# First modulation of a fused three-block network: two of its four units halved between VectorE and TensorE, its weight laid out by units

## The reference, cut to what matters

```
def _modulation(c, ada_w, ada_b):
    mod = jax.nn.silu(c) @ ada_w + ada_b            # c 1 x 1024, ada_w 1024 x 3072
    shift, scale, gate = jnp.split(mod[:, None, :], 3, axis=-1)
    return shift, scale, gate
...
h = _rmsnorm(x, norm_g[i]) * (1.0 + scale) + shift
proj = h @ w_in                                     # 512 x 1024 times 1024 x 4096
```

## Time and profile before

| | us |
|---|---|
| median of 3 runs | 1538.32 (1538.28 to 1540.69) |
| profiled execution, its own time | 1538.38 |
| span of that execution in the trace | 1536.5 |
| PE busy | 1382.3 (90% of the span) |
| DVE busy | 684.7 (45%) |
| ACT busy | 356.0 (23%) |
| POOL busy | 111.6 (7%) |
| moved by DMA | 338.08 MB, 220 GB/s over the span |

### The profile page before, as it was taken

The page is one execution under the profiler, slowest core; times in us unless marked ns, Lnnn a source line. Parts: engine busy times, 40 slices in busy tenths (PEclk is TensorE's granted clock), DMA queues, the critical chain, the costliest instruction groups (busy, mean ns, idle before and its releaser), DMA issues.

```text
span 1536.5 us, 17675 instructions
## 1 busy us (share of the span) xinstructions
PE 1382.3 (90%) x6712; PEld 699.3 (46%) x6712; DVE 684.7 (45%) x1313; ACT 356.0 (23%) x778; POOL 111.6 (7%) x227
## 2 busy tenths in 40 slices
PE   4999999999999999999999989979996968769685
PEld 2444444555464444664644445455443324223242
DVE  4675524884266723332599845263121112111125
ACT  2433204653220253431500154110000000000001
POOL 4000000010100000000200000112000001000003
PEclk9999999999999999999999989989998989989898
DMA  9763136004176741003424123169999999999995
GB/s 341 261 245 125 55 110 127 4 1 164 52 254 224 237 164 56 1 1 110 148 99 161 58 110 156 64 236 396 419 410 418 420 415 417 416 418 423 423 425 238
DMA packets 85133, 338.08 MB, mean 220 GB/s; under 512 B 10343, under 2 KB 16280, under 8 KB 72376
## 3 DMA queue, kind: packets, MB, share of 16 engines
q1 hardware_dynamic: 70752, 307.24, 51.5%
q0 software_dynamic: 5664, 13.70, 3.2%
q10 hardware_dynamic: 8632, 15.99, 2.9%
HBM read 323.34 MB, written 17.24 MB: 222 GB/s over the span
## 4 chain that ended last, share of the span: by engine, by line
PE 69%; DMA 15%; DVE 9%; issue 2%; ACT 2%; POOL 1%; DVEq 0%; SPq 0%; ACTq 0%; POOLq 0%
PE score_banks L723 14%; PE bank L734 13%; DMA slots<-in_w_exp_up 12%; PE score_banks L1214 9%; PE score_banks L734 5%; PE bank L1241 5%; PE bank L707 3%; PE bank L941 3%; PE score_banks L1228 2%; PE bank L896 2%; PE bank L1043 2%; PE score_banks L1034 2%; DVE bufD L2050 2%; PE score_banks L953 1%; PE bank L957 1%
## 5 line engine op out<-in xcount | busy, mean ns | idle before, releaser
L723 PE MATMUL score_banks<-slots 128*128 128x512 f32 (+1 forms) x584 | 243.3, 574 | 3.0 <-PE score_banks L723 1.5
L1214 PE MATMUL score_banks<-slots,norm_row 128*64 128x512 f32 (+1 forms) x672 | 147.2, 607 | 42.4 <-DMA slots<-in_w_exp_up 42.2
L734 PE MATMUL bank<-slots 128*128 128x512 f32 x416 | 183.2, 594 | 2.2 <-PE bank L734 0.9
L723 PEld LDWEIGHTS score_banks<-slots 128*128 128x128 f32 x584 | 110.4, 191 | 129.6 <-issue 126.8
L2540 DVE TENSOR_TENSOR mix<-probsT,score_banks 128x256 f32<-128x256 f32 (+1 forms) x39 | 14.4, 370 | 287.7 <-ACT probsT L1688 287.7
L1241 PE MATMUL bank<-slots,mix 128*64 128x512 f32 (+1 forms) x864 | 115.2, 477 | 12.0 <-issue 9.5
L734 PEld LDWEIGHTS bank<-slots 128*128 128x128 f32 x416 | 77.5, 190 | 96.6 <-issue 95.0
L1688 ACT ACTIVATE probsT<-score_banks 128x256 f32<-128x256 f32 (+1 forms) x39 | 13.4, 343 | 436.9 <-PE score_banks L1214 376.5
L1214 PEld LDWEIGHTS score_banks<-slots,norm_row 128*64 128x64 f32 (+1 forms) x672 | 49.9, 142 | 133.9 <-issue 132.5
L734 PE MATMUL score_banks<-slots 128*128 128x512 f32 (+1 forms) x256 | 95.2, 527 | 0.3 <-PE score_banks L734 0.3
L2427 DVE SCALAR_TENSOR_TENSOR bufD<-slots,col,bufD 128x512 f32<-128x512 f32 x120 | 80.5, 746 | 0.4
(11 more groups left out here) (376 smaller groups left out, 1767.4 us busy)
## 6 DMA issues: line engine op xcount, KB each, us to landing
slots<-in_w_exp_down SPq DMA_DIRECT2D x32, 2048.0 KB, 35.6
slots<-in_w_exp_gate SPq DMA_DIRECT2D x32, 2048.0 KB, 29.5
slots<-in_w_exp_up SPq DMA_DIRECT2D x32, 2048.0 KB, 34.7
slots<-in_w_in SPq DMA_DIRECT2D x16, 2048.0 KB, 9.0
slots<-in_w_mod SPq DMA_DIRECT2D x24, 1024.0 KB, 5.2
slots<-in_ada_w SPq DMA_DIRECT2D x18, 1024.0 KB, 6.4
slots<-in_w_out SPq DMA_DIRECT2D x6, 2048.0 KB, 8.2
slots<-in_ada_w SPq DMA_DIRECT2D x3, 2048.0 KB, 20.5
```

The lines of the kernel that those rows point to most:

```text
L723: last = mm(bank[:, cols], w[:, k, lo:lo + P], src[:, k, cols], start=(k == 0), stop=(k == kts - 1))
L734: last = mm(bank[:, 0:cols], features_k[:, t * P:(t + 1) * P], rhs(k), start=(k == 0), stop=(k == kts - 1))
L1214: last = mm(out, rows[:, k, :], e_gu[it.p][:, :, k, c * pc.ff:(c + 1) * pc.ff], start=(k == 0), stop=(k == KT - 1))
```

## The change

- On the host, ada_w0 (1024 x 3072) is laid out again as six units of 128 partitions x 8 rows x 512 columns, so that one partition's part of a unit is one run of 16 KB, and of a half unit one of 8 KB. No loads are added or taken away, and their order stays.
- Units 1 and 3 are halved: four of the eight rows on DVE, four on PE. PE's half (`half_unit`) takes the weight's 128x128 blocks as the stationary operand and silu(c)'s column as the one moving column: 16 matmuls, adding up over the four rows, into four columns of a bank. DVE's half is reduced as before, into four further columns of the same bank (`reduce_columns(bank, 4)`), and `take_halves` adds both and the bias with two DVE ops.
- `row_unit`, ACT's copy of the row and six of the 19 warming matmuls go.
- DVE weighs unit 0, four rows of unit 1, scales x, takes unit 0's columns, weighs unit 2 with the taking of unit 1 in its midst, then four rows of unit 3.
- `unit_used` goes up by one after unit 0, after unit 1 is taken and after unit 2 (before: one, then two at once). The first of the two steps of `mod_used` now comes from PE's half of unit 3, the second from DVE once that has been reached.

```diff
         def source(kind, u):
-            if kind in ("ada0", "ada1"):
-                w = a["ada_w0" if kind == "ada0" else "ada_w1"]
+            if kind == "ada0":
+                return a["ada_w0"][u]
+            if kind == "ada1":
+                w = a["ada_w1"]
                 return w[:, u * W:(u + 1) * W].rearrange("(p k) n -> p k n", p=P)
...
-            def reduce_columns():
+            def reduce_columns(bank=None, at=0):
...
-                pe.wait_ge(mod_summed, summed(n))
-                bank = dve_banks.claim(pe)
+                pe.wait_ge(mod_summed, n + 1)
+                bank = dve_banks.claim(pe) if bank is None else bank
                 for j in range(4):
-                    last = mm(bank[:, j:j + 1], mod_acc(n)[:, j * P:(j + 1) * P], ones[:, 0:1], start=True, stop=True)
+                    last = mm(bank[:, at + j:at + j + 1], mod_acc(n)[:, j * P:(j + 1) * P], ones[:, 0:1], start=True, stop=True)
...
-            def row_unit():
...
+            def half_unit(bank, rows, first):
+
+
                 for j in range(4):
-                    last = mm(bank[:, j:j + 1], mod_acc(1)[0:1, j * P:(j + 1) * P], ones[0:1, 0:1], start=True, stop=True)
-                last.then_inc(dve_filled, 1)
-                reduced[0] += 1
+                    for k in range(4):
+                        last = mm(bank[:, j:j + 1], rows[:, k, j * P:(j + 1) * P], silu_c[:, first + k:first + k + 1],
+                                  start=(k == 0), stop=(k == 3))
+                return last
...
             table_columns(0, R1_ROWS)
-            reduce_columns()
-            row_unit()
+            bank0, bank1 = dve_banks.claim(pe), dve_banks.claim(pe)
+            pe.wait_ge(silu_ready, 1)
+            pe.wait_ge(w_in[1], unit_arrival(1))
+            half_unit(bank1, unit_view(1)[:, 4:8], 4)
+            reduce_columns(bank0)
+            reduce_columns(bank1, 4)
             pe.wait_ge(xn_ready, TT)
             for k in range(KT):
                 transposes(act_banks, act_filled, [C_tok[:, t, k * P:(k + 1) * P] for t in range(TT)])
-            reduce_columns()
-            stay_warm(6)
-            reduce_columns()
+            bank2, bank3 = dve_banks.claim(pe), dve_banks.claim(pe)
+            pe.wait_ge(mod_in[0], 16)
+            half_unit(bank3, mod_half[0], 0).then_inc(mod_used, 1)
+            reduce_columns(bank2)
+            reduce_columns(bank3, 4)
             stay_warm(13)
...
             table_column(col1, R1_ROWS)
-            bank = tr_banks.take(act)
-            fn(mod_acc(1)[0:1, :], bank[0:1, :], ACT.Copy).then_inc(tr_freed, 1)
-            act.wait_ge(tr_freed, tr_banks.n)
-            act.sem_inc(row_copied, 1)
...
+            def weigh_second_unit():
+
+                dve.wait_ge(w_in[1], unit_arrival(1))
+                for k in range(4):
+                    chain(weigh_rows(1, k, unit_view(1)[:, k, :]))
+                dve.sem_inc(mod_summed, 1)
+
+            def weigh_third_unit(halfway):
+
+                dve.wait_ge(w_in[2], unit_arrival(2))
+                dve.wait_ge(mod_reduced, 1)
+                for k in range(KT):
+                    if k == 4:
+                        halfway()
+                    chain(weigh_rows(2, k, unit_view(2)[:, k, :]))
+                dve.sem_inc(mod_summed, 1)
+
+            def weigh_fourth_unit():
+
+                dve.wait_ge(mod_in[1], 16)
+                dve.wait_ge(mod_reduced, 2)
+                for k in range(4, KT):
+                    chain(weigh_rows(3, k, mod_half[1][:, k - 4, :], first=4))
+                dve.sem_inc(mod_summed, 1)
+                halves_done[0] = 2
...
+            def take_halves(n, layer, u, bias_col):
+
+                bank = dve_banks.take(dve)
+                part = mods[layer][:, 4 * u:4 * u + 4]
+                chain(v.tensor_tensor(part, bank[:, 0:4], col1[:, bias_col + 4 * u:bias_col + 4 * u + 4], ALU.add))
+                v.tensor_tensor(part, bank[:, 4:8], part, ALU.add).then_inc(dve_freed, 1)
                 dve.wait_ge(dve_freed, dve_banks.n)
                 dve.sem_inc(mod_reduced, 1)
...
             dve.wait_ge(silu_ready, 1)
-            weigh_unit(0)
+            weigh_first_unit()
             dve.sem_inc(unit_used, 1)
+            weigh_second_unit()
             scale_x(0)
             dve.wait_ge(act_freed, 1)
             take_columns(0, 0, 0, R1["ada_b0"])
-            weigh_unit(2)
-            take_columns(1, 0, 1, R1["ada_b0"])
-            dve.sem_inc(unit_used, 2)
-            weigh(3)
+
+            def second_unit_done():
+
+                take_halves(1, 0, 1, R1["ada_b0"])
+                dve.sem_inc(unit_used, 1)
+
+            weigh_third_unit(second_unit_done)
+            dve.sem_inc(unit_used, 1)
+            weigh_fourth_unit()
             take_columns(2, 0, 2, R1["ada_b0"])
-            take_columns(3, 0, 3, R1["ada_b0"])
+            take_halves(3, 0, 3, R1["ada_b0"])
+            dve.wait_ge(mod_used, 1)
+            dve.sem_inc(mod_used, 1)
             affine(0, R1["norm_g0"], col1)
...
+    given["ada_w0"] = np.ascontiguousarray(given["ada_w0"].reshape(P, KT, 3 * D // W, W).transpose(2, 0, 1, 3))
```

More of the change, by code:

```diff
@@ L283, in mod_acc @@
             return buf[:, lo + n % 2 * W:lo + (n % 2 + 1) * W]
-        def summed(n):
-            return n if n > 0 else 1
         def c_loads():
@@ L327, in fused_kernel @@
         mod_in = [sem(f"mod_half_loaded{i}") for i in range(2)]
-        row_copied = sem("second_unit_row_copied")
         mod_used, mod_summed, mod_reduced = sem("mod_half_used"), sem("mod_unit_summed"), sem("mod_unit_reduced")
@@ L2043, in _, with weigh_rows, weigh_first_unit @@
             sums_done, halves_done = [0], [0]
-            def weigh_rows(n, k, w):
+            def weigh_rows(n, k, w, first=0):
                 c = silu_c[:, (0 if n < 12 else 8) + k:(0 if n < 12 else 8) + k + 1]
                 acc = mod_acc(n)
-                if k == 0:
+                if k == first:
                     return v.tensor_scalar(acc, w, c, None, ALU.mult)
                 return v.scalar_tensor_tensor(out=acc, in0=w, scalar=c, in1=acc, op0=ALU.mult, op1=ALU.add)
[L2052 to L2056, removed]
+            def weigh_first_unit():
+                dve.wait_ge(w_in[0], unit_arrival(0))
                 for k in range(KT):
-                    chain(weigh_rows(n, k, unit_view(n)[:, k, :]))
+                    chain(weigh_rows(0, k, unit_view(0)[:, k, :]))
                 dve.sem_inc(mod_summed, 1)
+            def weigh_second_unit():
[18 more added lines that the diff above has]
+                halves_done[0] = 2
             def weigh_half(n, half):
@@ L2083, in take_columns @@
                                 ALU.add).then_inc(dve_freed, 1)
+                dve.wait_ge(dve_freed, dve_banks.n)
+                dve.sem_inc(mod_reduced, 1)
+            def take_halves(n, layer, u, bias_col):
[3 more added lines that the diff above has]
+                v.tensor_tensor(part, bank[:, 4:8], part, ALU.add).then_inc(dve_freed, 1)
                 dve.wait_ge(dve_freed, dve_banks.n)
```

## The result

The changed kernel takes 1554.56 us (median of 4 runs, 1553.32 to 1555.46) against 1538.30 beside it: ratio 1.0114, interval 1.0102 to 1.0126. It is slower, by 16.3 us between the medians. The forecast was 1554, with a range of 1545 to 1563.

The account below looks back on a forecast made before the run. The start-up chain before PE's projection at 45.85 us was in play. A bias table at 33.0, then PE's steps and warming, put the projection at 61.7, 15.9 later: 1538.38 + 15.9 = 1554.3, taken as 1554, range 1545 to 1563.

Parts of the forecast that it names:

- Turns by record: Load queues SP and ACT alternate record by record, so 16 KB ada_w0 records delay the bias table from 19.43 to 33.0.
- its two bounds: Margins on the bias table's landing at 33.0 us: -2.0 and +1.5.
- Unit 0 early, and worth nothing: Unit 0's weight lands at about 10 us, without gain, as DVE weighs until about 20, then waits to scale x.
- PE's clock: PE's one-column work: 1.2 GHz for the first half unit and reductions, rising mid-transposes; 7.5 us, then 4.2 per half unit.
- such a fall: Clock falling in one-column work before the 13 warming matmuls, reaching to 62.8; half of 2.2, 1.1 us, was added.
- Cover: Beside PE's first half unit and reductions: x's squares, root and scaling end at 38.0 to 41.1, before the first reduction's 42.9.
- the forecast's fourth rival: Start-up loads as now but a slow PE clock: projection at 50.2, +4.3, 1542.7 us; chance 8%.
- The end: From the last reduction through warming to PE's first projection (win0): start at 61.7 us, 15.9 later than before.
- The forecast's premise: From 45.85 us PE's projection is the chain, so whatever moves its start moves the kernel's end by as much.
- the third rival: PE's clock stays at 1.2 GHz through transposes and halves: projection +23.7, 1562 to 1566 us; chance 14%.

Follow-up runs that it names:

- e3: The changed kernel with x's load moved from ACT's queue to SP's, right behind unit 0: 1542.32 us, ratio 1.0025 to the kernel before.
- e7: The changed kernel with ada_w0 laid out by pairs of rows, so 4 KB records in place of 16: 1545.80 us, ratio 1.0055 to the kernel before.
- e4: e3 with seven added 512-column matmuls, results unread, five before the first half unit and one after each: 1545.45 us, ratio 1.0039 to the kernel before.
- e9: The changed kernel with ada_w0's old 2 KB layout, x behind unit 0 on SP's queue, six unread 512-column matmuls in PE's wait: 1541.17 us, ratio 1.0035.
- e2: The changed kernel with ada_w0's old layout (2 KB records), so the halves alone: 1540.67 us, ratio 1.0025 to the kernel before.
- e10: e6 with 16 in place of 6 warming matmuls ahead of the last reduction: 1538.79 us, ratio 1.0012 to the kernel before.
- e6: The kernel before with x's load alone moved from ACT's queue to SP's, behind unit 0: 1536.75 us, ratio 0.9998 to the kernel before.

## Why the prediction was right

**Turns by record.** Right, and shown twice over: by the counts in the changed kernel and by 2, 4 and 16 KB records giving the table at 19.3, 25.6 and 34.6 us. The forecast of 33.0 for the table was 1.6 short (34.64, just past the upper of its two bounds); x at 29.6 lay inside 27.6 to 30.7. Two parts were counted too short. Of the two c loads only the second was counted, but both took turns, 128 each, beside units 0 and 1, so the last of x met win0's records. And the table's small records at the end were counted as one for one with SP's, which they were not: from 32 to 34.6 us 466 of SP's went with 111 of ACT's, and e3 and e7 show the same.

**Unit 0 early, and worth nothing.** Right in its effect and wrong in the reason's detail: unit 0 was weighed from 14.5 and not from about 10, since c_2, which its weighing needs as well, landed only at 14.2. The forecast had set its records beside unit 0's but no time for their landing.

**PE's clock.** Right in the first part, wrong in the second. It was taken as 1.2 GHz for half of unit 1 and its reductions, with a rise in the midst of the transposes and 2.4 after. The steps, forecast and measured: half unit 7.5 and 6.64, reductions 3.7 and 3.41, transposes 5.6 and 5.96, second half unit 4.2 and 4.45, its reductions 2.1 and 3.41, from there to the projection 5.05 and 5.28. Only the second reductions are far off, by 1.3 us: the clock fell again within the second half unit. The forecast had weighed such a fall, at half its price, for the warming matmuls alone. The first half unit came out shorter because a record took 0.21 us and not the 0.234 read from a reduction of eight. Before, the clock had risen during the long matmuls of L841, which the change took away; e4 and e9 show long matmuls raising it.

**Cover.** Right: x's squares, root and scaling ended before the first reductions did, and DVE was never late. In the changed kernel PE waits for nothing from 34.77 on. What e2 adds: the forecast's fourth rival, loads as now and a slow clock, priced at +4.3, came out at 1.6 us at the projection and 2.8 between the medians, as the clock rose in it too.

**The end.** The projection was forecast at 61.7 and came at 64.36, 2.7 us late: 1.7 in the table's arrival and transpose, 1.3 in the second reductions and 0.8 in the other steps, less 1.2 in the first half unit and its reductions. The rest of the span took 1.3 us less than before, so the median is within 0.6 us of the forecast and the profiled execution within 1.2. That close an agreement is luck. The forecast's premise that a later start of the projection moves the end by as much holds only to a few us: in e3 the start is 2.1 us later and the median 4.5, in e9 5.6 and 4.3, and in e10 the start is 0.3 earlier and the median 1.9 later.

The rule of the Trainium skill ("TensorE: Matmul & The Clock Gate", Part 4) that transposes don't count as activity stood for the third rival. Here the trace disagrees: the clock rose at 50 us with PE doing nothing but transposes for the 4.8 us before.

## What to carry to other kernels

In these runs, as long as two DMA queues both had many records waiting, each record bought the other queue one record. Enlarging one stream's records then takes bandwidth from whatever loads share the time, so ask first what those loads hold up. Putting the large one of them behind the first weight on the same queue gave most of the loss back here. Before moving a matrix-vector product to one-column matmuls, look at what raised TensorE's clock, as it may be the very work that goes. And price a start-up stage by what lands last, not by the engine that was busiest in it.

## What the runs showed that was not expected

- A load of 4 KB (c_2, 128 records of 32 bytes) landed at 14.2 us beside 16 KB records, 9 us later than before: beside large records its time went by its number of records, not its bytes.
- Warming matmuls can become the path: at the lower clock the last 13 took 5.28 us in the changed kernel, 4.64 in e6, and held back a projection whose input had been ready for 1.4 and 1.1 us.
- Half units of one form took 6.96 and 3.47 us in one and the same execution (e2), at the lower and at the higher clock.
